# Load and input projection in one program, from unnormalised x, in split fp32r products

## The chip, the cores and the metric

One core of a Trainium2 chip runs the whole kernel in one launch. The metric is the device time of that launch in microseconds, lower is better. TensorE (PE) multiplies; DVE, ACT and POOL are the vector, scalar and GpSimd engines; SP issues transfers.

## The reference, cut to what matters

The kernel computes one decoder layer (attention with three branches beside a state space model, then a gated convolution FFN) for 1024 prompt tokens and 8 sample tokens, all in fp32. The change touches what stands first, the norm and the one input projection of all 1032 tokens:

```python
def rmsnorm(x, g):
    xf = x.astype(jnp.float32)
    y = xf * lax.rsqrt(jnp.mean(xf * xf, axis=-1, keepdims=True) + EPS)
    return (y * g.astype(jnp.float32)).astype(x.dtype)

def project_in(h, w_in):
    z = h @ w_in          # 1024 rows; columns: q 512, kv_c 256, kv_s 256, kv_w 256, gates 24, u 512
...
h = rmsnorm(x, p['norm_mix'])
q, kvc_rows, kvs_rows, kvw_rows, gl, u = project_in(h, p['w_in'])
```

The key/value rows are also results (p_kv_cmp, p_kv_sel, p_kv_win and the same of the samples). Everything after the projection (compression of keys and values, attention, state space scan, output projection, FFN, final norm) is computed by later stages, which the change leaves alone but for the places that they read from.

## The kernel before

The kernel is a row of programs (`nc.Block`), each ending with all engines before the next begins: stage_load, stage_project, stage_compress, stage_attend, stage_turn_attention, stage_ssm, stage_ffn, stage_results (build, at the end). Engines wait on counting semaphores. Each engine's instructions, and each transfer queue's, run in the order in which they are written; nothing is planned by a program.

stage_load: SP loads x in two transfers of 4 token tiles. PE turns each tile of 128 tokens in eight transposes (L184) into PSUM; ACT (L161) and DVE (L204) copy the halves to xT, which holds x with features on the partitions. ACT sums the squares of each token (Square with accumulator, L163), DVE adds and inverts, ACT takes one root for all tiles (Mean.root, L253). Vectors (norms, convolution weights) are turned in L193 and L195.

stage_project: PE spreads the factor of each token over all partitions (Scaling.multiply, L316), ACT keeps it (L322), and DVE makes mixT = xT * gain * factor in eight instructions (Scaling.scale, L328). The jobs then run in the order of JOBS: four query blocks (`q`, weights stationary, three chunks of 344 tokens moving, L473), nine jobs of keys, values and gates (`kv`, tokens stationary, 2 x 396 columns moving, L478), nine of u (`u`, every eighth token stationary, 2 x 256 columns moving, L484). All products are plain fp32. PSUM banks alternate between two groups of four, and ACT and DVE evict half of each job (L588, L531 to L544), so PE waits for the job before the last. Between the jobs the parameters of the state space model are made: small fp32 work on DVE after each eviction (factors, chunk_powers, phases, inputs, weigh_inputs, turns, outputs), the turns of Cin (L495) and Bw (L505) and the kernels K (L519) on PE. SP loads the weights of q and of kv in one transfer each, writes xT to DRAM (x_kept, which the output projection adds later), loads u's weights into the place of q's when the queries are done, and stores the key/value rows tile by tile. E_early, Bw, CW_early and K are spilled to DRAM.

stage_compress: PE turns u (L904), ACT and DVE move it, SP spills it. PE turns rows of the cache (L887) and multiplies them by w_cmp (L896), ACT and DVE move each fill between the two. The rows of a sample come by an indirect transfer from POOL (L877) into one of two tile buffers; the second fetch waits for the spill of u.

The FFN already works with split fp32r products: ACT rounds an operand to fp32r ("upper"), DVE or POOL subtract it from the full value ("rest"), and three products high*high, high*low and low*high stand for one fp32 product (L2455, and L2074 in the state space stage).

## Time and profile before

| | us |
|---|---|
| median of 3 runs (1859.19 to 1865.96) | 1862.39 |
| span of the profiled execution | 1862.2 |
| PE busy | 1730.0 (93%) |
| DVE busy | 942.1 (51%) |
| ACT busy | 564.6 (30%) |
| POOL busy | 351.0 (19%) |
| x turned, PE's first transpose | 9.16 |
| first projection matmul | 36.64 |
| first instruction of PE in stage_compress | 275.03 |

The profile is of one execution. Busy time is the union of an engine's instructions; PEld is the loading of stationary operands, which runs beside the matmuls. A matmul's own duration contains its way through the array, so a stream is read by the distance from start to start, not by the duration of one. An fp32 matmul is recorded as two matmuls.

### The profile page before, as it was taken

Reading aid. Unit: us, or ns where it says so; the run is one execution under the profiler, and the core shown is the slowest. Engines: PE = TensorE matmul, PEld = TensorE weight load, DVE = VectorE, ACT = ScalarE, POOL = GpSimd, SP = SyncE. Lnnn points to the kernel's source line nnn. Section 1 sums busy time; section 2 is a strip of 40 time slices with the busy share of each in tenths; the row PEclk is TensorE's granted clock in tenths of the full one; section 3 lists DMA queues with packets and bytes.
Section 4 is the critical chain, followed back from the end, with each engine's and each line's share of the span. In section 5 each row is a group of like instructions: output and inputs, shape, how many; then the busy total and the mean of one; then the engine's idle time right before and its main releaser. Section 6 shows DMA issues by size and latency. Waiting matters only on the chain. (4 is left out here: it accounts for less than half of the span.)

```text
span 1862.2 us, 27167 instructions
## 1 busy us (share of the span) xinstructions
PE 1730.0 (93%) x10863; PEld 1490.2 (80%) x10864; DVE 942.1 (51%) x1593; ACT 564.6 (30%) x876; POOL 351.0 (19%) x288
## 2 busy tenths in 40 slices
PE   5999999969989998878979899999999999999988
PEld 4655788956555554547979899999999999999978
DVE  3356216776553444119231455655565566556544
ACT  4001115645443444211132332222232222222232
POOL 0000100042213121212125022222222222222210
PEclk8999999979999999797989899999999999999988
DMA  6312516412326134354040111211112112111102
GB/s 241 70 63 77 222 32 227 176 57 62 102 64 214 57 93 179 119 168 148 4 128 1 42 34 40 62 34 59 42 34 68 34 34 68 34 46 55 34 12 97
DMA packets 90684, 155.15 MB, mean 83 GB/s; under 512 B 15302, under 2 KB 68078, under 8 KB 88254
## 3 DMA queue, kind: packets, MB, share of 16 engines
q1 hardware_dynamic: 76736, 93.13, 15.6%
q0 software_dynamic: 13056, 59.77, 9.8%
q10 hardware_dynamic: 816, 1.18, 0.2%
q8 instruction: 54, 0.88, 0.2%
q14 instruction: 22, 0.18, 0.0%
HBM read 133.61 MB, written 24.83 MB: 85 GB/s over the span
## 5 line engine op out<-in xcount | busy, mean ns | idle before, releaser
L2455 PE MATMUL ps<-h_up,w_split 128*128 128x344 f32 x2112 | 399.5, 321 | 7.1 <-DVE h_rest L2617 5.2
L2627 DVE TENSOR_TENSOR xT<-ps,xT 128x688 f32<-128x688 f32 x352 | 228.2, 690 | 283.3 <-PE ps L2455 268.3
L2455 PEld LDWEIGHTS ps<-h_up,w_split 128*128 128x128 f32 x2112 | 345.0, 189 | 8.9 <-DVE h_rest L2617 4.2
L2455 PE MATMUL ps<-gated,wd_split 128*128 128x344 f32 x1584 | 258.3, 321 | 0.9 <-ACT last_row L2569 0.9
L2455 PEld LDWEIGHTS ps<-gated,wd_split 128*128 128x128 f32 x1584 | 251.0, 188 | 1.6 <-issue 1.1
L2455 PE MATMUL ps<-h_rest,w_split 128*128 128x344 f32 x1056 | 224.8, 321 | 0.4 <-ACT wd_split L2565 0.4
L2455 PEld LDWEIGHTS ps<-h_rest,w_split 128*128 128x128 f32 x1056 | 179.1, 189 | 0.7 <-ACT wd_split L2565 0.7
L2581 POOL TENSOR_TENSOR w_split<-w_raw,w_split 128x1024 fp32r<-128x1024 f32 x44 | 114.3, 2598 | 152.4 <-ACT w_split L2527 152.4
L2541 ACT ACTIVATE hu<-ps 128x1032 f32<-128x1032 f32 x44 | 45.4, 1033 | 314.5 <-PE ps L2455 314.5
L2635 DVE SCALAR_TENSOR_TENSOR cv<-hu,ccol,cv 128x1024 f32<-128x1024 f32 x88 | 129.5, 1472 | 16.4 <-ACT cv L2543 10.7
L1719 DVE TENSOR_REDUCE top<-ps 128x1 f32<-128x384 f32 (+4 forms) x124 | 71.1, 585 | 108.1 <-PE ps L1302 63.2
L478 PE MATMUL ps<-w_kvg,mixT 128*128 128x396 f32 (+1 forms) x288 | 96.8, 497 | 0.0
L1623 POOL DMA_INDIRECT unit<-in_cache_kv_sel,rows x64 | 61.1, 955 | 188.1 <-PE ps L1404 97.6
L2602 POOL TENSOR_TENSOR wd_split<-wd_raw,wd_split 128x1024 fp32r<-128x1024 f32 x22 | 54.9, 2496 | 165.5 <-ACT wd_split L2565 165.5
L478 PEld LDWEIGHTS ps<-w_kvg,mixT 128*128 128x128 f32 (+1 forms) x288 | 51.2, 179 | 42.8 <-issue 7.8
L1302 PEld LDWEIGHTS ps<-kT,q_up 128*128 128x128 f32 x336 | 61.5, 201 | 22.6 <-DVE top L1719 6.7
L1302 PE MATMUL ps<-kT,q_up 128*128 128x128 f32 (+3 forms) x336 | 72.7, 306 | 7.1 <-DVE top L1719 2.9
L896 PE MATMUL ps<-rowsT,w_c 128*128 128x128 f32 (+1 forms) x576 | 76.3, 276 | 1.6 <-ACT rowsT L965 1.3
L1335 PE MATMUL ps<-q_up,kT 128*128 128x512 f32 x132 | 69.9, 529 | 3.3 <-ACT prob_win L1543 2.3
L896 PEld LDWEIGHTS ps<-rowsT,w_c 128*128 128x128 f32 x576 | 69.8, 192 | 3.4 <-issue 3.4
L945 DVE COPY rowsT<-ps 64x256 f32<-64x256 f32 (+1 forms) x144 | 59.4, 413 | 22.2 <-PE ps L887 20.1
L484 PE MATMUL ps<-w_qu,mixT 128*128 128x256 f32 (+1 forms) x288 | 70.1, 404 | 0.0
(459 smaller groups left out, 2576.4 us busy)
## 6 DMA issues: line engine op xcount, KB each, us to landing
w_raw<-in_w_up SPq DMA_DIRECT2D x44, 512.0 KB, 6.2
wd_raw<-in_w_down SPq DMA_DIRECT2D x22, 512.0 KB, 3.6
unit<-in_cache_kv_win POOLq DMA_DIRECT2D x16, 512.0 KB, 4.5
x_kept<-xT SPq DMA_DIRECT2D x1, 4128.0 KB, 25.2
xT<-x_kept SPq DMA_DIRECT2D x1, 4128.0 KB
xtok<-in_x_prompt SPq DMA_DIRECT2D x2, 2048.0 KB, 8.2
w_qu<-in_w_in SPq DMA_DIRECT2D x2, 2048.0 KB, 8.7
w_out_sb<-in_w_out SPq DMA_DIRECT2D x4, 1024.0 KB, 11.1
```

What stands on the lines that cost most here:

```text
L478: mm = pe.matmul(k.ps[0:n, bank + c, 0:KVH], hT[:, a, t * P:t * P + n], k.w_kvg[:, a, c * KVH:(c + 1) * KVH], **on)
L484: mm = pe.matmul(k.ps[0:n, bank + c, 0:256], tokens, k.w_qu[:, a, c * 256:c * 256 + 256], **on)
L896: mm = pe.matmul(k.ps[:, 4 + 2 * (j % 2) + h, x * P:x * P + n], k.w_c[:, x, 2 * quad + a].rearrange("p r e -> p (r e)"), k.rowsT[:, f % 4, ...
L945: ins = copy(k.rowsT[HD * s2:HD * s2 + HD, f % 4, h, :, 0:n], rows[:, s2, :, 0:n])
L1302: mm = pe.matmul(out, k.q_up[:, g % 2, h0 + h, :], k.kT[:, br, kvh, b0 * P:(b0 + nb) * P], start=True, stop=b0 not in masks)
L1335: pe.matmul(out, first, k.q_up[:, g % 2].rearrange("p h q -> p (h q)"), start=True, stop=False)
L1623: pool.indirect_dma_start(unit, None, pages, bass.IndirectOffsetOnAxis(ap=k.rows4[:, f, NH2 * n + bb:NH2 * n + bb + 1], axis=0)).then_inc( ...
L1719: dve.tensor_reduce(to, s, AX.X, ALU.max).then_inc(reduced, 1)
L2455: mm = pe.matmul(k.ps[:, bank + c, 0:TG], w(wn), x(xn)[:, c * TG:c * TG + TG], start=start and m == 0, stop=stop and m == 2)
L2581: pool.tensor_tensor(k.w_split[:, z, 1], k.w_raw[:, z], k.w_split[:, z, 0].bitcast(F32), ALU.subtract).then_inc(w_rest, 1)
L2627: dve.tensor_tensor(x[:, part], k.ps[:, bank + part.start:bank + part.stop, 0:TG], x[:, part], ALU.add).then_inc(added, 1)
L2635: dve.scalar_tensor_tensor(k.cv[:, z, 0:SEQ], k.hu[:, z, 1 - n:SEQ + 1 - n], w, k.cv[:, z, 0:SEQ], ALU.mult, ALU.add)
```

## The change

stage_load and stage_project become one program, stage_front. x is loaded tile by tile. When a tile is turned, ACT rounds it from PSUM to fp32r (xh) and DVE subtracts that from PSUM (xl); no xT and no mixT are made. The norm is split: its gain (vcol) goes into the weights, which ACT scales and rounds ("upper") and DVE or POOL complete ("lower"); the factor of each token goes into the evictions, as a scale by partition for kv and u and as a product with the spread factor for the queries. Each tile has its own Square, Sqrt (now with EPS as bias) and reciprocal. Each projection is three fp32r products. Keys and values are cut into three branches of 256, 256 and 280 columns, each over all tiles; the first begins after two tiles are turned, and the turns of the others stand between its jobs. u follows, in one bank of 512 columns a job, with four jobs begun on the first half of the weights; the queries are last. Weight slices share four places, so each is loaded when the branch before that used the place is done. ACT evicts kv and u alone, DVE the queries alone. POOL sums xh and xl and writes the sum to x_kept, eight times, and makes some of the lower parts. DVE makes the state space parameters in one run after the first branch. kv rows are stored four tiles at a time, the window copy of the cache follows the kernels K. stage_compress gets three tile buffers, and its fetches no longer wait for the spill of u. Offsets change, and later stages read kv without the first branch, which has a place of its own (kvc).

```diff
+    R = [k.off_tmp + 8960 * n for n in range(4)]
+
+    def pair(name, parts, width, high, low):
+        hi, _ = at(f"{name}_hi", [P, parts, width], F32R, high)
+        lo, _ = at(f"{name}_lo", [P, parts, width], F32R, low)
+        raw, _ = at(f"{name}_raw", [P, parts, width], F32, low)
+        return hi, lo, raw
+    k.w_kv = [pair(f"w_kv{c}", KD, WIDE[c], R[2 * (c % 2)], R[2 * (c % 2) + 1]) for c in range(3)]
+    k.w_u = [pair(f"w_u{n}", KD // 2, SSMW, R[(2, 0)[n]], R[(3, 1)[n]]) for n in range(2)]
+    q_at = (k.off_kv, R[0], R[1], R[0])
+    k.w_q = [pair(f"w_q{m}", KD, P, q_at[m], q_at[m] + 4096) for m in range(NSAW // P)]
+    k.x_sum, o = at("x_sum", [P, TOK], F32, R[3] + 8960)
+    assert o <= k.off_tail, o
...
+    KV_JOBS = [(c, t) for c in range(3) for t in range(NT + 1)]
+    FIRST_U = len(KV_JOBS)
+    FIRST_Q = len(KV_JOBS) + CH + 1
+    U_BANKS = (0, 1, 2, 4, 5, 6, 0, 1, 2)
+    AHEAD = 4
+    SHORT_AT, C_AT = (0, 5), (1, 0)
+    BT_AT = {(2, x): (2 * x, 2 * x + 1) for x in range(BT_FILLS // 2)}
+    KK_AT = {4 + x: x for x in range(KK_FILLS)}
...
+            xv = k.dram["x_prompt"][0].rearrange("(t p) d -> p t d", p=P)
+
+            def x_tile(t):
+                sp.dma_start(k.xtok[:, t], xv[:, t]).then_inc(x_loaded[t], 16)
+            x_tile(0)
+            for n in range(2):
+                sp.dma_start(k.w_kv[0][2][:, 4 * n:4 * n + 4], wv[:, 4 * n:4 * n + 4, CUT_KV:CUT_KV + KVW]).then_inc(w_in["kv", 0, n], 16)
+            for t in range(1, NT):
+                x_tile(t)
+            sp.dma_start(k.xs[:], k.dram["x_sample"].rearrange("b s d -> (b s) d")).then_inc(x_loaded[NT], 16)
+            sp.dma_start(k.w_kv[1][2][:], wv[:, :, CUT_KV + KVW:CUT_KV + 2 * KVW]).then_inc(w_in["kv", 1, 0], 16)
...
+            sp.wait_ge(left, 4)
+            rows(0, 0, cmp_out)
+            sp.wait_ge(left, 8)
+            rows(0, 4, cmp_out)
+            sp.wait_ge(projected, 9)
+            sp.dma_start(k.w_kv[2][2][:], wv[:, :, CUT_KV + 2 * KVW:CUT_U]).then_inc(w_in["kv", 2, 0], 16)
+            sp.wait_ge(left, 9)
+            sample_rows(0, first_rows)
+            sp.wait_ge(scaling.kept, 1)
+            sp.dma_start(rs_kept, scaling.factor[0:1, 0:SEQ]).then_inc(rs_out, 16)
+            sp.wait_ge(rs_out, 16)
+            sp.dma_start(k.rstd_u[:], rs_kept.rearrange("o (n t) -> (o n) t", t=CH)).then_inc(rs_back, 16)
...
+            sp.wait_ge(projected, 18)
+            sp.dma_start(k.w_u[0][2][:], wv[:, 0:4, CUT_U:CUT_U + SSMW]).then_inc(w_in["u", 0, 0], 16)
...
+            sp.wait_ge(projected, 27)
+            sp.dma_start(k.w_u[1][2][:], wv[:, 4:8, CUT_U:CUT_U + SSMW]).then_inc(w_in["u", 1, 0], 16)
             sp.wait_ge(e_made, 1)
             sp.dma_start(k.e_kept, k.E_early[:].rearrange("p n j c -> p (n j c)")).then_inc(k.e_out, 16)
+            sp.wait_ge(*k.cmp_rows_stored)
+            sp.wait_ge(first_rows, 16)
+            sp.dma_start(k.w_q[0][2][:], wv[:, :, 0:P]).then_inc(w_in["q", 0, 0], 16)
...
+            pe.wait_ge(const_made, 2)
+            turn_x(0)
...
+            turn_x(1)
+            for j, (c, t) in enumerate(Front.KV_JOBS):
+                if c == 0 and t + 2 <= NT:
+                    turn_x(t + 2)
+                if j >= 3:
+                    pe.wait_ge(left, j - 2)
+                if c == 0:
+                    pe.wait_ge(xh_made, min(2 * t + 2, 2 * NT + 1))
+                    pe.wait_ge(xl_made, min(2 * t + 2, 2 * NT + 1))
+                elif t == 0:
+                    pe.wait_ge(w_high, Front.highs("kv", c))
+                    pe.wait_ge(w_low_dve if c == 1 else w_low_pool, Front.lows("kv", c))
...
+                        pe.wait_ge(w_high, a + 1)
+                    tokens, rest = k.xh[:, a, t * P:t * P + n], k.xl[:, a, t * P:t * P + n]
+                    out = k.ps[0:n, j % 3, 0:WIDE[c]]
+                    pe.matmul(out, tokens, high[:, a], start=(a == 0), stop=False)
+                    pe.matmul(out, rest, high[:, a], start=False, stop=False)
+                    if j == 0:
+                        pe.wait_ge(w_low_dve, a + 1)
+                    mm = pe.matmul(out, tokens, low[:, a], start=False, stop=(a == KD - 1))
                 mm.then_inc(projected, 1)
...
+                if (c, t) == (0, NT):
+                    pe.wait_ge(inverted, NT + 1)
+                    scaling.multiply(pe)
...
+            def project_u(t, n):
...
+                    d = 4 * n + a
+                    if t == 0 and n == 1:
+                        pe.wait_ge(w_high, Front.highs("u", 0) + a + 1)
+                        pe.wait_ge(w_low_pool, Front.lows("u", 0) + a + 1)
+                    tokens, rest = [x[:, d, t:SEQ:CH] if t < CH else x[:, d, SEQ:TOK] for x in (k.xh, k.xl)]
+                    pe.matmul(out, tokens, high[:, a], start=(d == 0), stop=False)
+                    pe.matmul(out, tokens, low[:, a], start=False, stop=False)
+                    mm = pe.matmul(out, rest, high[:, a], start=False, stop=(d == KD - 1))
...
+            pe.wait_ge(w_high, Front.highs("u", 0))
+            pe.wait_ge(w_low_pool, Front.lows("u", 0))
+            for t in range(Front.AHEAD):
+                pe.wait_ge(left, Front.FIRST_U - 2 + t if t < 3 else Front.FIRST_U)
+                if t == 3:
+                    pe.wait_ge(scaling.kept, 1)
+                project_u(t, 0)
+            for t in range(CH + 1):
+                if t >= Front.AHEAD:
+                    if t >= 6:
+                        pe.wait_ge(left, Front.FIRST_U + t - 5)
+                    project_u(t, 0)
+                project_u(t, 1).then_inc(projected, 1)
...
+            for m in range(Front.NQ):
+                bank = 4 * (1 - m % 2)
+                high, low, _ = k.w_q[m]
+                pe.wait_ge(w_high, Front.highs("q", m))
+                pe.wait_ge(w_low_dve, Front.lows("q", m))
+                if m < 2:
+                    pe.wait_ge(left, Front.FIRST_U + (6 if m == 0 else CH + 1))
+                else:
+                    pe.wait_ge(q_left, m - 1)
+                for a in range(KD):
+                    for n, (w, x) in enumerate(((high, k.xh), (high, k.xl), (low, k.xh))):
+                        for c in range(3):
+                            mm = pe.matmul(k.ps[:, bank + c, 0:TG], w[:, a], x[:, a, c * TG:c * TG + TG],
+                                           start=(a == 0 and n == 0), stop=(a == KD - 1 and n == 2))
+                mm.then_inc(projected, 1)
...
+            act.wait_ge(ldt_in, 48)
+            act.activation(k.ldt[:], k.ldt[:], ACT.Exp).then_inc(sined, 1)
+            act.wait_ge(to_sine, 1)
+            act.activation(k.PA[:, MAG], k.PA[:, X], ACT.Exp).then_inc(sined, 1)
+            act.wait_ge(to_sine, 2)
+            act.activation(k.PA[:, SIN], k.PA[:, T2], ACT.Sin)
+            act.activation(k.PA[:, T1], k.PA[:, T2], ACT.Sin, scale=0.5).then_inc(sined, 1)
...
+            def root(t):
+                n, x = (P, k.xtok[:, t]) if t < NT else (NB, k.xs[:])
+                act.wait_ge(x_loaded[t], 16)
+                act.activation(k.square[0:n], x, ACT.Square, scale=D_MODEL ** -0.5, accum_out=k.stat[0:n, 0, t:t + 1]).then_inc(summed, 1)
+                act.wait_ge(summed, t + 1)
+                act.activation(k.stat[0:n, 1, t:t + 1], k.stat[0:n, 0, t:t + 1], ACT.Sqrt, bias=k.eps[0:n]).then_inc(rooted, 1)
+
+            def upper(kind, n):
+                high, _, raw = {"kv": k.w_kv, "u": k.w_u, "q": k.w_q}[kind][n]
+                first = KD // 2 * n if kind == "u" else 0
+                for a in range(KD // 2 if kind == "u" else KD):
+                    if a == 0:
+                        act.wait_ge(w_in[kind, n, 0], 16)
+                    if (kind, n) == ("kv", 0) and a == KD // 2:
+                        act.wait_ge(w_in["kv", 0, 1], 16)
+                    act.activation(high[:, a], raw[:, a], ACT.Copy, scale=k.vcol[:, first + a:first + a + 1]).then_inc(w_high, 1)
+                    if kind == "u":
+                        act.activation(raw[:, a], raw[:, a], ACT.Copy, scale=k.vcol[:, first + a:first + a + 1]).then_inc(w_scaled, 1)
+
+            def leave(j, out, src, factor):
+                act.wait_ge(projected, j + 1)
+                act.activation(out, src, ACT.Copy, scale=factor).then_inc(left, 1)
...
+            upper("kv", 0)
+            take_x(1)
+            root(0)
+            act.activation(k.ccol[:], k.ps[:, 7, 32:32 + 8 * NF].rearrange("p (a b) -> p a b", a=4), ACT.Copy).then_inc(vt_kept, 1)
+            for j, (c, t) in enumerate(Front.KV_JOBS):
+                if c == 0:
+                    if t + 2 <= NT:
+                        take_x(t + 2)
+                    if t + 1 <= NT:
+                        root(t + 1)
+                    act.wait_ge(inverted, t + 1)
+                n = P if t < NT else NB
+                to = k.kvc[0:n, t] if c == 0 else k.kv[0:n, t, (c - 1) * KVW:(c - 1) * KVW + WIDE[c]]
+                leave(j, to, k.ps[0:n, j % 3, 0:WIDE[c]], k.stat[0:n, 3, t:t + 1])
+                if (c, t) == (0, 6):
+                    upper("kv", 1)
+                if (c, t) == (0, NT):
+                    scaling.keep(act)
+                if (c, t) == (1, 3):
+                    act.wait_ge(projected, 9)
+                    upper("kv", 2)
...
+                if (c, t) == (2, 4):
+                    upper("u", 0)
+            upper("u", 1)
+            for t in range(CH + 1):
+                j, src = Front.FIRST_U + t, k.ps[0:(P if t < CH else NB), Front.U_BANKS[t], :]
+                if t == 0:
+                    act.wait_ge(k.e_out, 16)
+                    act.wait_ge(rs_back, 16)
+                if t < CH:
+                    leave(j, k.U[:, :, CH - 1 - t, :], src.rearrange("p (g c) -> p g c", c=GC), k.rstd_u[:, t:t + 1])
+                else:
...
+                if t == 3:
+                    upper("q", 0)
...
+            for m in range(1, Front.NQ):
+                if m == 3:
+                    act.wait_ge(projected, Front.FIRST_Q + 2)
+                act.dma_start(k.w_q[m][2][:], wv[:, :, m * P:m * P + P]).then_inc(w_in["q", m, 0], 16)
+                if m == 2:
+                    for n in (1, 2):
+                        upper("q", n)
+            upper("q", 3)
...
+            def lower_kv():
+                high, low, raw = k.w_kv[2]
+                pool.wait_ge(w_high, Front.highs("kv", 2))
+                for a in range(KD):
+                    pool.tensor_scalar(raw[:, a], raw[:, a], k.vcol[:, a:a + 1], None, ALU.mult).then_inc(lane_made, 1)
+                for a in range(KD):
+                    pool.wait_ge(lane_made, a + 2)
+                    pool.tensor_tensor(low[:, a], raw[:, a], high[:, a].bitcast(F32), ALU.subtract).then_inc(w_low_pool, 1)
+
+            def lower_u(n):
+                high, low, raw = k.w_u[n]
+                for a in range(KD // 2):
+                    pool.wait_ge(w_scaled, 4 * n + a + 1)
+                    pool.tensor_tensor(low[:, a], raw[:, a], high[:, a].bitcast(F32), ALU.subtract).then_inc(w_low_pool, 1)
+
+            def keep_x(a):
+                pool.wait_ge(xl_made, 2 * NT + 1)
+                if a:
+                    pool.wait_ge(x_spilled, 16 * a)
+                pool.tensor_tensor(k.x_sum[:], k.xh[:, a].bitcast(F32), k.xl[:, a].bitcast(F32), ALU.add).then_inc(x_summed, 1)
+                pool.wait_ge(x_summed, a + 1)
+                pool.dma_start(k.x_kept[:, a * TOK:a * TOK + TOK], k.x_sum[:]).then_inc(x_spilled, 16)
+            for a in range(3):
+                keep_x(a)
+            lower_kv()
+            for a in range(3, 6):
+                keep_x(a)
+            lower_u(0)
+            for a in range(6, KD):
+                keep_x(a)
+            lower_u(1)
             pool.wait_ge(cw_made, 1)
...
-                                      ).then_inc(kk_added, 1)
-            for a in range(KD):
...
+            def lower(kind, n):
+                high, low, raw = (k.w_kv if kind == "kv" else k.w_q)[n]
+                for a in range(KD):
+                    dve.wait_ge(w_high, Front.highs(kind, n) - KD + a + 1)
+                    dve.scalar_tensor_tensor(low[:, a], raw[:, a], k.vcol[:, a:a + 1], high[:, a].bitcast(F32),
+                                             ALU.mult, ALU.subtract).then_inc(w_low_dve, 1)
...
             angles()
-            leave(dve, dve.tensor_copy, 1, left_dve, after)
-    k.rows_stored = (rows_out, n_rows_out[0])
-    k.stores.append(k.rows_stored)
+            take_x_rest(0)
+            lower("kv", 0)
+            take_x_rest(1)
+            invert(0)
+            for n in range(NT + 1):
+                if n + 2 <= NT:
+                    take_x_rest(n + 2)
+                if n + 1 <= NT:
+                    invert(n + 1)
+                if n in (1, 2, 3):
+                    factors(n - 1)
+            lower("kv", 1)
+            chunk_powers()
+            phases()
+            inputs()
+            weigh_inputs(0)
+            weigh_inputs(1)
+            for first, last in ((0, 3), (3, 5), (5, 6), (6, 7)):
+                turns(first, last)
+            outputs(0)
+            outputs(1)
...
+            dve.wait_ge(scaling.kept, 1)
+            lower("q", 1)
+            lower("q", 2)
...
+    k.tile = [at(f"tile{n + 1}", [P, SUB, 2 * NKV, HD], F32, (k.off_mix, k.off_mix + 16384, 9216 + 16384)[n])[0] for n in range(3)]
...
+                if j >= 4:
+
+                    pool.wait_ge(transposed, FILLS * (j - 2))
+                pool.indirect_dma_start(k.tile[b % 3][:].rearrange("n s c d -> n (s c d)"), None, rows,
```

## Rows read from the trace of the kernel before

**Rows 1.** By stretch: length, busy PE, PEld, DVE, ACT, POOL; clock, transfer share, GB/s.

```profile
20.00:36.60 16.60, 3.74 (x19) 3.50 (x18) 4.00 (x5) 10.10 (x17) 0.12 (x1) 0.63 0.46 159
36.60:97.40 60.80, 60.76 (x231) 40.20 (x231) 25.83 (x79) 6.39 (x9) 0.00 (x0) 0.96 0.44 126
97.40:197.00 99.60, 99.60 (x322) 54.81 (x321) 63.02 (x116) 8.57 (x16) 0.93 (x2) 1.00 0.24 90
197.00:275.00 78.00, 77.25 (x417) 70.49 (x417) 6.37 (x18) 8.18 (x18) 4.75 (x7) 1.00 0.33 116
```

**Rows 2.** Timeline of TensorE before 50 us: start, length, what, count.

```profile
9.16 9.51 PE L184 MATMUL ps<-ident,xtok 128*128 128x128 f32 x64 [9.16 <-DMA xtok<-in_x_prompt]
...
36.64 2.09 PE L473 MATMUL ps<-mixT,w_qu 128*128 128x344 f32 x3 [4.76 <-DMA w_qu<-in_w_in]
```

**Rows 3.** Timeline of TensorE, the projections, to the start of stage_compress.

```profile
67.40 28.03 PE L473 MATMUL ps<-mixT,w_qu 128*128 128x344 f32 x96
95.36 2.16 PE L495 MATMUL ps<-ident,Cin 16*128 16x16 f32 x32
...
129.47 1.04 PE L505 MATMUL ps<-ident,Bw 128*128 128x128 f32 x8
130.34 10.81 PE L478 MATMUL ps<-w_kvg,mixT 128*128 128x396 f32 x32
...
206.81 8.02 PE L484 MATMUL ps<-w_qu,mixT 128*128 128x256 f32 x32
...
216.62 8.02 PE L484 MATMUL ps<-w_qu,mixT 128*128 128x256 f32 x32
...
236.23 38.02 PE L484 MATMUL ps<-w_qu,mixT 128*128 128x256 f32 x160
275.03 3.68 PE L904 MATMUL ps<-ident,U 128*128 128x128 f32 x32 [0.78 <-PEq L393]
```

**Rows 4.** Timeline of TensorE, fp32r products in attention and in the gated unit.

```profile
459.94 0.39 PE L1339 MATMUL ps<-q,k 128*128 128x512 f32 x1
460.17 0.34 PE L1302 MATMUL ps<-kT,q_up 128*128 128x256 f32 x2
...
901.11 0.63 PE L2074 MATMUL ps<-g_rest,w_glu_up 128*128 128x344 f32 x3
901.58 0.62 PE L2074 MATMUL ps<-g_up,w_glu_rest 128*128 128x344 f32 x3
```

**Rows 5.** Timeline of TensorE in stage_compress: turns and products of one fill.

```profile
296.06 1.06 PE L896 MATMUL ps<-rowsT,w_c 128*128 128x128 f32 x8
296.95 0.60 PE L887 MATMUL ps<-ident,tile 128*128 128x128 f32 x4
297.39 1.06 PE L896 MATMUL ps<-rowsT,w_c 128*128 128x128 f32 x8
```

**Rows 6.** Weight loads of u by shape: count, busy us, mean ns, idle before.

```profile
L484 PEld LDWEIGHTS ps<-w_qu,mixT 128*128 128x128 f32 x256 | 61.6, 337 | 1.5 <-issue 1.5
```

**Rows 7.** Groups of ACT by shape: count, busy us, mean ns, idle before.

```profile
L163 ACT ACTIVATE square<-xtok 128x1024 f32<-128x1024 f32 x8 | 8.4, 1049 | 0.0
...
L161 ACT ACTIVATE xT<-ps 128x512 f32<-128x512 f32 x8 | 4.8, 598 | 0.2
...
L253 ACT ACT_TABLE_LOAD x3 | 3.8, 1283 | 0.1
```

**Rows 8.** Groups of DVE by shape: the eviction of the queries.

```profile
L531 DVE COPY qT<-ps 64x1032 f32<-64x1032 f32 x4 | 4.9, 1234 | 32.1 <-PE ps L473 32.1
```

**Rows 9.** Groups of POOL by shape: a subtraction of 512 columns.

```profile
L1578 POOL TENSOR_TENSOR q<-qT,q_up 64x512 fp32r<-64x512 f32 x16 | 20.2, 1262 | 83.3 <-ACT q_up L1471 83.1
```

**Rows 10.** Page, transfers: count, KB each, median us to landing.

```profile
unit<-in_cache_kv_win POOLq DMA_DIRECT2D x16, 512.0 KB, 4.5
...
w_qu<-in_w_in SPq DMA_DIRECT2D x2, 2048.0 KB, 8.7
```

**Rows 11.** Waits, 275 to 382 us: us in total, times, longest.

```profile
PE ps L887 <- DMA tile<-in_cache_kv_cmp,rows_of: 3.0, 2, 1.9
```

669 lines of the change are left out of this document (301 added, 368 removed).

## The prediction

> **What bounds the kernel now.** I read the busy time by stretch first [rows 1]. Only the time before 275 us is touched in earnest. There TensorE is the bound: from 36.6 to 275 us it is busy for 237.6 of 238.4 us, while DVE, ACT and POOL are mostly idle. Before that it mostly waits: from 20 to 36.6 us it is busy for 3.7 us, and its clock is there partly at the lower of its two levels (1.2 of 2.4 GHz), for the mean granted clock is 0.63. Second, the timeline of TensorE [rows 2] names what those 36.6 us are: x turned from 9.16 us on, then the norm's factor, the scaled copy mixT, and a wait for w_qu. The first projection matmul is at 36.64. Third, the timeline of the projections [rows 3] gives pitches. The evictions lie beside them: jobs follow each other without a gap. The attention, the output projection and the FFN keep their instructions, so I leave their time alone.
>
> So the front costs 275.0 us, from the start to TensorE's first instruction of stage_compress [rows 3], and I build the same interval for the changed kernel. The profiled span, 1862.2 us, is 0.2 us below the median of the runs, 1862.4, so one sum serves for both.
>
> **Prices.** A plain fp32 product is recorded as two matmuls, each with two passes. The 344 wide one takes 28.03/96 = 0.292 us a record, the 396 wide one 10.81/32, some 0.335, and the 256 wide one of the u part 38.8/160, some 0.24 us (236.23 to 275.03) [rows 3]. Split fp32r products replace each of them with three matmuls of one pass. Three fp32r matmuls of 344 columns start 0.47 us apart, 0.157 each, and one of 512 columns is followed by the next after 0.23 us [rows 4]. Both are 0.45 to 0.46 ns a column, so I take 0.12 us for 256 columns and 0.131 for 280. The lower bound is 0.111, the pitch of matmuls with as much streaming (128 columns in two passes) and a weight load each [rows 5]: 8 of them in 0.89 us. The upper bound is 0.13.
>
> The u part has a stride of 8 tokens in its stationary operand. Its weight load is 337 ns long [rows 6], and by the 396 wide records its 256 wide ones should take 0.335 x 256/396 = 0.217 us, but they take 0.24. I read the strided load as the bound there, and I keep 0.24 us for the 512 wide fp32r matmul, which alone would need 0.23. Its bounds are 0.23 and 0.28.
>
> The Trainium skill puts a weight load at the number of columns over 1.2 GHz, some 107 ns, whatever the stride (TensorE: Matmul & The Clock Gate, section LDWEIGHTS). By that page the u part would be bound by its columns and cost 2 us less. This trace speaks against it, with 337 ns against 107, so the sum doesn't use it.
>
> **The change part by part.**
> First job ready. x tile 0 is now a transfer of 0.5 MB, not 2, so its turns begin near 5 us instead of 9.16. But the small vectors and the ssm parameters come over ACT's queue (11 issues, the last near 5.5 us), and ACT does Exp, Exp, Sin, Sin before it takes tile 0. I put the first scaled weight slice at 12.5 us (bounds 10 and 16); ACT and DVE then deliver a slice each 0.45 us, so job 0 ends near 16.5. The 28 us of norm, mixT and weight wait ahead of the first product are gone: the norm's factor is only needed at the evictions.
>
> First branch (kvc). Job 1 starts near 17.5, when ACT has taken tile 1. A job has 24 matmuls of 0.12, 2.9 us, and the turns of a later tile, 8 x 0.11 = 0.9 us [rows 5]: 3.8 us. ACT has per tile two takes, a Square with its accumulator, a Sqrt and an eviction: 2 x 0.6 + 1.05 + 0.19 + 0.3 + 0.45, some 3.2 us [rows 7]. So TensorE is just the bound. Jobs 1 to 5 take 19, job 6 3.5, job 7 2.9, the job of 8 samples 2.7, and the parameter turns 0.5: the branch ends at 46.
>
> Spreading the factor, 18 records at the upper clock: 2. Second branch: 8 x 2.88 + 2.7 = 25.7, and the 32 turns of Cin 2.1 [rows 3]. Third branch, 280 wide: 8 x 3.14 + 3.1 = 28.2. The turns of Bw cost 0.87 a pair of fills (129.47 to 130.34), 3.5 in all; they are moved, not new. The u part: 192 x 0.24 + 24 x 0.23 = 51.6, and four kernel fills of 2.15 (a u job with its fill starts 9.81 after the one before, from 206.81 to 216.62, and 32 records of 0.24 are 7.66), 8.6 [rows 3]. The queries: 4 x 72 x 0.158 = 45.5; these were 56 and cost four fifths now. At the end DVE alone evicts the last queries, two instructions of 1.23 [rows 8], and the program's end adds 0.4: 3.0, where before it was 0.8.
>
> Sum: 46 + 2 + 25.7 + 2.1 + 28.2 + 3.5 + 51.6 + 8.6 + 45.5 + 3.0 = 216.2.
>
> Seams. Each weight slice is loaded, scaled and split before its branch, and I follow each. For the third branch ACT has the upper part at 66 us. POOL then scales and subtracts 8 slices; at 1262 ns for 512 columns [rows 9] that is 0.7 each for the subtraction, and 0.3 to 0.7 for the scaling: it ends at 74 to 78, needed at 76. For the second half of u the load starts only when job 27 ends. 2 MB took 8.7 us and 0.5 MB 4.5 [rows 10], so it lands after 5 to 8; its four slices need 2.5 more for the first and 1.3 for each that follows. The four u jobs run ahead on the first half cover 11.5: nothing, or up to 3. For query block 1 the load goes out on ACT's queue with the 4 MB copy of the window cache in flight; block 0 covers it for 11.4 us: 0 to 5. POOL's new work (eight sums of x of 2.5 us, each with a transfer waited for, 7 us a piece) lies ahead of its splits on its queue. It begins near 38 us and is clear of them by 56, so it costs nothing while that cover holds; if each took 12 us the last split would be 4 us late. DVE's parameter work (63 us busy of 99.6 from 97.4 on, evictions included [rows 1], and some 10 before) loses its evictions and runs unbroken from 45 us: Bw by 73 us (needed at 79), CW by 118 (needed at 145). SP's waits in order (for jobs 9, 18, 27) hold nothing that is needed sooner. I add 1.5 us for the seams, bounds 0 and 12.
>
> stage_compress. With three tile buffers the fetches no longer wait for the spill of u; TensorE's waits for tiles are 3.0 us [rows 11]. I take 2 of them back (bounds 3 and -1).
>
> Result: 275.0 - 216.2 - 1.5 + 2 = 59.3 us less, **1803 us**.
>
> **Rivals.**
> Table loads. Sqrt now stands between Squares, tile by tile. The trace shows a load of 1283 ns before each Sqrt [rows 7]; it shows Square and Copy under three different tables without a load, and Copy under Sqrt's, but never Square under Sqrt's. If Square isn't there, ACT has two loads per tile, 5.8 us against TensorE's 3.8: 2 us for each of 7 or 8 tiles, 15 us, **1818 us**. Square's use under each other table speaks against it: 12%.
> The Trainium skill says to finish all calls of one table set before the next, and counts cheap functions as members of every set without naming Square (ScalarE: Activation LUTs, section Table sets: the hidden batching unit). Its rule, applied to the letter, is this rival.
>
> Late splits. POOL's sums of x, POOL's slower scaling, and the loads that start only at a branch's end are each at the bad bound: 4 + 3 + 5 us and less cover from one to the next. TensorE then stands at the starts of the third branch, the second half of u and query block 1. That is 10 us over the forecast, **1813 us**: 13%.
>
> Clock. TensorE is now fed by ACT and DVE tile by tile, and in this trace a stretch with such gaps ran at a mean of 0.63 [rows 1]. At the lower level all pitches double. The gain is gone when 59 us of matmul time run there, that is all of the first branch (27 us) and the second and a part of the third. Fully kept up to the end of the third branch, 27 + 26 + 28 us are added to the forecast: **1884 us**, slower than before. Against it: branches two and three wait for no tile, and the timeline shows the upper level soon after the products start (0.96 from 36.6 on): 3%.
>
> The change doesn't do what it says: three matmuls of one pass cost no less than two records of two passes if the pitch were bound by the load. For 256 columns this is already nearly so (24 x 0.12 for 256 columns against 32 x 0.335 for 792); with 0.14 instead of 0.12 the kv part would cost 8 us more, 1811 us, inside the range.
>
> **How the numbers follow.** The forecast, 1795 to 1813 on its own, has 69%, table loads 12%, late splits 13%, the clock 3%, and 3% is for what I don't see. The range takes in the first three with their bounds: **1795 to 1824**. A measurement of this kernel can tell 0.3%, 5.6 us, from no change. Faster by more than that: 0.95; within it: 0.02; slower: 0.03.
>
> **What would show it.** TensorE's first instruction of the compression stage at 216 to 220 us, not 275. Pitches of 0.12 (256 columns), 0.24 (u) and 0.158 (queries). ACT's table loads before 60 us: three, or some twenty. TensorE's idle time before the first matmul of the third branch, of u's second half and of query block 1: near nothing. If the stages behind 275 us change by more than 3 us in all, something that I left alone has moved. I am wrong if the first job ends after 22 us, if the u part costs more than 65 us with its fills, or if the granted clock is below 0.9 between 20 and 100 us.

## The result, and the profile after

The changed kernel takes 1857.45 us (median of 14 runs, 1850.79 to 1864.63), the kernel before 1864.16 us in the same sessions (14 runs). The ratio is 0.9963, with a 95% interval of 0.9953 to 0.9974: some 7 us less, where 59 us less were forecast. The forecast of 1803 us and its range of 1795 to 1824 us are both wrong. The profiled execution has a span of 1853.9 us, against 1862.2 us before.

TensorE's first instruction of stage_compress is at 268.44 us (before: 275.03, rows 3; forecast: 217.7, that is 216.2 and 1.5 for the seams). What lies behind it is 1585.5 us long, against 1587.2. So the missing gain is all in the front, and most of it lies in three waits and in the lower clock behind them. The waits of TensorE ahead of 275 us, in the changed kernel (us in total, times, longest):

```profile
PE ps L548 <- ACT w_q_hi L596: 19.3, 1, 19.3
PE ps L477 <- POOL w_kv_lo L703: 11.1, 1, 11.1
PE ps L514 <- POOL w_u_lo L709: 6.9, 4, 5.2
PE ps L453 <- DMA crow<-in_conv_b: 5.7, 1, 5.7
PE ps L425 <- DMA xtok<-in_x_prompt: 4.8, 1, 4.8
PE ps L1095 <- PEq L323: 2.8, 1, 2.8
PE ps L477 <- DVE w_kv_lo L894: 1.4, 1, 1.4
```

L477 is the first product of a kv job, L514 that of a u job, L548 the queries, L1095 the first turn of stage_compress. The same stretch by windows (length, busy TensorE, granted clock, transfer share, GB/s), which answers to rows 1:

```profile
80.00:100.00 20.00, 8.91 (x51) 0.66 0.31 106
100.00:140.00 40.00, 37.26 (x249) 1.00 0.52 191
140.00:160.00 20.00, 15.84 (x44) 0.66 0.54 169
...
200.00:220.00 20.00, 10.31 (x66) 0.82 0.67 216
220.00:240.00 20.00, 10.44 (x55) 0.67 0.26 49
```

A stretch of 20 us mixes the wait with what follows it. In stretches of 5 us (length, busy TensorE, granted clock, transfer share, GB/s) the work behind the waits is seen by itself:

```profile
90.00:95.00 5.00, 3.69 (x16) 0.50 0.02 6
...
150.00:155.00 5.00, 5.00 (x13) 0.52 0.88 324
155.00:160.00 5.00, 5.00 (x22) 1.00 0.98 242
```

From 230 to 235 us, behind the third wait, the granted clock is 0.67, and from 235 us on 1.00. So each of the three waits is followed by a stretch at the lower clock. How it looks in the timeline of TensorE (start, length, what, count, idle time before and its releaser), at the edges of the stretches:

```profile
48.49 2.33 PE L211 MATMUL ps<-ident,stat 128*128 128x128 f32 x18
52.25 0.36 PE L477 MATMUL ps<-w_kv_hi,xh 128*128 128x256 f32 x1 [1.43 <-DVE w_kv_lo L894]
...
91.31 0.57 PE L477 MATMUL ps<-w_kv_hi,xh 128*128 128x280 f32 x1 [11.09 <-POOL w_kv_lo L703]
...
125.23 0.51 PE L514 MATMUL ps<-w_u_hi,xh 128*128 128x512 f32 x1
...
198.79 0.63 PE L548 MATMUL ps<-xh,w_q_hi 128*128 128x344 f32 x3
...
229.56 1.20 PE L548 MATMUL ps<-xh,w_q_hi 128*128 128x344 f32 x3 [19.25 <-ACT w_q_hi L596]
...
234.66 0.64 PE L548 MATMUL ps<-xl,w_q_hi 128*128 128x344 f32 x3
```

From these edges the forecast's sum can be settled term by term:

| stretch | forecast | measured | over |
|---|---|---|---|
| start to the end of the first branch | 46 | 48.49 | 2.5 |
| factor spread, to branch 2 | 2 | 3.76 | 1.8 |
| branch 2 with Cin (to 80.22) | 27.8 | 27.97 | 0.2 |
| wait before branch 3 | in the seams | 11.09 | 11.1 |
| branch 3 with Bw | 31.7 | 33.92 | 2.2 |
| u with the kernel fills | 60.2 | 73.56 | 13.4 (6.9 idle) |
| queries and end | 48.5 | 69.65 | 21.1 (19.3 idle) |

The excess is 52.2 us, less the 1.5 us that the forecast had for seams: 50.7. Waits in the seams are 37.3 of it. What is left in the last three rows beside their waits is 2.2 + 6.5 + 1.8 = 10.5 us. Of it 1.4 are u's own price (in e10_kk_later, below, where the clock stays up, u takes 62.7 us with 1.1 of wait, 1.4 over the forecast); 9.1 lie at the lower clock behind the waits. 4.4 us are ahead of all that; 1.4 of them are TensorE's wait for DVE's lower part of the second branch, for which the forecast had no term.

### The profile page after: what moved, and what is told of

Read it like the earlier page. It is cut to its first block and busy times, and to the rows that moved or that the text cites. A ratio compares the mean times of both kernels' runs of the same rounds, so it can differ in the third digit from the quotient of the medians.

```text
span 1853.9 us, 28106 instructions
## 1 busy us (share of the span) xinstructions
PE 1692.8 (91%) x11248; PEld 1513.0 (82%) x11248; DVE 976.0 (53%) x1635; ACT 604.5 (33%) x978; POOL 412.8 (22%) x328
## 3 DMA queue, kind: packets, MB, share of 16 engines
q1 hardware_dynamic: 78610, 87.32, 15.3%
q0 software_dynamic: 14208, 64.00, 10.3%
## 5 line engine op out<-in xcount | busy, mean ns | idle before, releaser
L1493 PEld LDWEIGHTS ps<-kT,q_up 128*128 128x128 f32 x336 | 62.0, 202 | 23.4 <-DVE top L1910 6.4
L477 PE MATMUL ps<-w_kv_hi,xh 128*128 128x256 f32 (+3 forms) x216 | 64.2, 297 | 12.5 <-POOL w_kv_lo L703 11.1
L2776 POOL COPY last<-hu 128x10 f32 (+1 forms) x44 | 8.5, 192 | 292.1 <-ACT hu L2732 292.1
L1526 PE MATMUL ps<-q_up,kT 128*128 128x512 f32 x132 | 70.1, 531 | 3.1 <-ACT prob_win L1734 2.3
L2752 ACT ACTIVATE gated<-cv 128x1032 fp32r<-128x1032 f32 x22 | 23.5, 1070 | 148.4 <-DVE cv L2844 148.4
L1136 DVE COPY rowsT<-ps 64x256 f32<-64x256 f32 (+1 forms) x144 | 59.4, 413 | 20.3 <-PE ps L1078 18.3
## 6 DMA issues: line engine op xcount, KB each, us to landing
w_out_sb<-in_w_out SPq DMA_DIRECT2D x4, 1024.0 KB, 11.1
```

Of the source, the lines that this page charges most:

```text
L477: pe.matmul(out, tokens, high[:, a], start=(a == 0), stop=False)
L1136: ins = copy(k.rowsT[HD * s2:HD * s2 + HD, f % 4, h, :, 0:n], rows[:, s2, :, 0:n])
L1493: mm = pe.matmul(out, k.q_up[:, g % 2, h0 + h, :], k.kT[:, br, kvh, b0 * P:(b0 + nb) * P], start=True, stop=b0 not in masks)
L1526: pe.matmul(out, first, k.q_up[:, g % 2].rearrange("p h q -> p (h q)"), start=True, stop=False)
```

## The experiments

All edits are made to the changed kernel; times are compared with the kernel before, run on the same chip. The clearest measure is where stage_compress starts in the profile, since what lies behind it differs little (1582.5 to 1592.8 us in all but e12_warm_all, where it is 1603.8). Where a kernel has one run, its time alone settles little: the changed kernel's 14 runs lie up to 7 us from their median. The starts are of one profile each, and the wait in u differs between kernels whose edit doesn't touch it (6.9, 7.0 and 8.2 us, but 3.4 in e9_late_crow and 4.1 in e1_copy_early). So a start is put down to an edit only as far as the wait that the edit aims at has changed.

| kernel | start | wait, branch 3 | wait, u | wait, queries | new waits | median (ratio, interval) |
|---|---|---|---|---|---|---|
| changed | 268.4 | 11.1 | 6.9 | 19.3 | | 1857.5 (0.9963, 0.9953 to 0.9974) |
| e1_copy_early | 247.6 | 10.4 | 4.1 | 0 | bt_stage 5.1 | 1838.8 (0.9865, 0.9833 to 0.9897) |
| e2_tile0_late | 260.3 | 10.4 | 6.9 | 12.1 | | 1847.2, one run |
| e11_copy_behind | 251.7 | 10.2 | 8.2 | 2.6 (block 3) | | 1840.7, one run |
| e3_split_dve | 249.1 | 0 | 0.2 | 19.0 | Bw 4.3, CW 0.5 | 1838.4 (0.9875, 0.9837 to 0.9914) |
| e4_act_scales | 250.0 | 5.1 | 0.7 | 18.3 | | 1840.4, one run |
| e5_dve_quiet | 265.3 | 3.7 | 0 | 19.1 | Bw 15.3 | 1859.8, one run |
| e6_pool_order | 259.7 | 10.2 | 2.2 | 19.5 | | 1846.5 (0.9905, 0.9873 to 0.9937) |
| e9_late_crow | 261.8 | 10.9 | 3.4 | 19.5 | | 1846.4, one run |
| e7_warm | 267.7 | 2.1 | 7.0 | 19.4 | | 1857.1 (0.9949, 0.9932 to 0.9966) |
| e12_warm_all | 259.4 | 0.4 | 0 | 1.3 | | 1856.8 (0.9955, 0.9935 to 0.9975) |
| e8_three | 230.4 | 0 | 0.9 | 0 | CW 6.2 | 1817.8 (0.9750, 0.9722 to 0.9777) |
| e10_kk_later | 223.2 | 0 | 1.1 | 0 | | 1811.1 (0.9739, 0.9716 to 0.9763) |

### The wait before query block 1

SP issues the 4 MB copy just before the loads of w_q1 and w_q2. SP's and ACT's timelines in the changed kernel:

```profile
195.10 0.82 SPq L399 DMA_DIRECT2D out_s_kv_win<-in_cache_kv_win  x1
...
201.74 13.15 SPq L407 DMA_DIRECT2D tile<-out_p_kv_cmp  x1
```

```profile
199.00 1.05 ACTq L664 DMA_DIRECT2D w_q_raw<-in_w_in  x2
226.63 2.45 ACT L596 ACTIVATE w_q_hi<-w_q_raw,vcol 128x128 fp32r<-128x128 f32 x8 [26.96 <-DMA w_q_raw<-in_w_in]
```

The 512 KB of w_q1 need 27.6 us, where 512 KB took 4.5 us in rows 10. SP's own instruction for the tile's fetch takes 13.15 us here, and 0.54 in e1_copy_early, where the copy isn't just ahead of it. Three orders of the same transfers were tried.

e1_copy_early:

```
             sample_rows(1, rows_out)
+            sp.dma_start(k.dram["s_kv_win"][0, :, 0:WIN - 1].rearrange("b t a h d -> b t (a h d)"),
+                         k.dram["cache_kv_win"][0, :, 1:WIN].rearrange("b t a h d -> b t (a h d)")).then_inc(cache_out, 16)
...
-            sp.dma_start(k.dram["s_kv_win"][0, :, 0:WIN - 1].rearrange("b t a h d -> b t (a h d)"),
-                         k.dram["cache_kv_win"][0, :, 1:WIN].rearrange("b t a h d -> b t (a h d)")).then_inc(cache_out, 16)
             sp.wait_ge(projected, Front.FIRST_Q)
```

> Edit to the changed kernel: SP issues the 4 MB copy of the window cache behind the store of the samples' second rows (near 81 us) and not behind the last kernel store (195 us). Theory 'copy': in the changed kernel the load of w_q1, issued at 199.0 us, lands at 226.6 us because the copy, issued at 195.1, is ahead of it on the same 16 DMA engines. Then w_q1 now lands 4 to 8 us after its issue, TensorE's idle time of 19.3 us before query block 1 falls to 0 to 3, and the block runs at the full clock from its start (1.5 to 2 us more). Together 18 to 22 us less than the changed kernel: 1836 to 1840 us, a ratio of 0.985 to 0.987 to the kernel before. Rival 'tile': the 1 MB fetch of the first tile of stage_compress (issued at 201.7) and its small pe_cmp rows are what w_q1 shares the engines with; then it still lands after 15 us or more, the idle time stays above 10, and the gain is under 10 us. Second rival 'moved': the copy, now beside the load of w_u0, the x sums' spills and bt's stores, costs as much there, in the third branch or the first half of u; then the query seam is gone and the time is not less.

e2_tile0_late:

```
-            sp.wait_ge(projected, Front.FIRST_Q)
+            sp.wait_ge(projected, Front.FIRST_Q + 3)
```

> Edit to the changed kernel: SP waits for three query blocks, not for the last u job, before it fetches the first tile of stage_compress (four pe_cmp loads and 1 MB of rows). The copy of the window cache stays where it is. Theory 'copy': w_q1 still lands 12 us or more after its issue and TensorE still waits 5 us or more before query block 1. Rival 'tile': w_q1 lands 4 to 8 us after its issue, the idle time is 0 to 3, and the time falls by 18 to 22 us. In between, if both loads share the engines evenly with w_q1: landing after 14 to 18 us, idle 6 to 10, which would say that the 27 us were the sum of both. The tile itself is needed near 250 to 268 us and comes in time if it lands within 10 us.

e11_copy_behind:

```
-            sp.dma_start(k.dram["s_kv_win"][0, :, 0:WIN - 1].rearrange("b t a h d -> b t (a h d)"),
-                         k.dram["cache_kv_win"][0, :, 1:WIN].rearrange("b t a h d -> b t (a h d)")).then_inc(cache_out, 16)
             sp.wait_ge(projected, Front.FIRST_Q)
...
                          k.dram["p_kv_cmp"][0, 0].rearrange("(n s) x h d -> n (s x h d)", s=SUB)).then_inc(k.prompt_in, 16)
+            sp.dma_start(k.dram["s_kv_win"][0, :, 0:WIN - 1].rearrange("b t a h d -> b t (a h d)"),
+                         k.dram["cache_kv_win"][0, :, 1:WIN].rearrange("b t a h d -> b t (a h d)")).then_inc(cache_out, 16)
```

> Edit to the changed kernel: the copy of the window cache is issued behind the fetch of the first tile, near 202 us, so that the loads of w_q1 and w_q2 (issued at 199.0) are in the queues ahead of it. Theory 'ahead': a load waits for what was given to the same 16 DMA engines before it, not for what comes after. Then w_q1 lands 4 to 8 us after its issue though the copy runs at the same time, the 19.3 us of wait before query block 1 are gone, and the time falls by 15 to 22 us. Rival 'beside': the engines divide themselves between all queues, so that w_q1 again lands 12 us or more after its issue whenever the copy is in flight. w_q3, issued near 222, may land late by the copy's rest in both cases (up to 5 us before block 3).

ACT's first split of w_q1 in e1_copy_early, in e2_tile0_late and in e11_copy_behind, with its wait for the load, and in the first and the last of them also that of w_q2, whose load was issued 0.45 us behind w_q1's:

```profile
203.47 2.46 ACT L596 ACTIVATE w_q_hi<-w_q_raw,vcol 128x128 fp32r<-128x128 f32 x8 [3.40 <-DMA w_q_raw<-in_w_in]
207.60 2.46 ACT L596 ACTIVATE w_q_hi<-w_q_raw,vcol 128x128 fp32r<-128x128 f32 x8 [1.68 <-DMA w_q_raw<-in_w_in]
```

```profile
218.54 3.61 ACT L596 ACTIVATE w_q_hi<-w_q_raw,vcol 128x128 fp32r<-128x128 f32 x12 [19.81 <-DMA w_q_raw<-in_w_in]
```

```profile
203.34 2.45 ACT L596 ACTIVATE w_q_hi<-w_q_raw,vcol 128x128 fp32r<-128x128 f32 x8 [3.57 <-DMA w_q_raw<-in_w_in]
207.65 2.45 ACT L596 ACTIVATE w_q_hi<-w_q_raw,vcol 128x128 fp32r<-128x128 f32 x8 [1.86 <-DMA w_q_raw<-in_w_in]
```

With the copy issued at 82 us, w_q1 lands 4.1 us after its issue, in the company of the tile's fetch. With the copy ahead and the tile's fetch out of the way it takes 20.5 us; the fetch adds 7. With the copy issued 3.4 us behind it, it takes 4.2 us; but then it had only 0.8 us to go, so this says little against 'beside'. The load of w_q2 says more: it had 5.2 us to go when the copy was issued, and landed after 8.1 us, against 7.7 in e1_copy_early. So for these loads 'ahead' holds and 'beside' falls: what counts is what was issued before. The third load, w_q3, shows the same from the other side: in e11_copy_behind it is issued 19.3 us behind the copy and takes 11.0 us, against 3.7 to 3.8 in the others. Whether a load behind the copy moves nothing until the copy is through, or only a small share, these runs do not tell. 'moved' came true in part: in e1_copy_early bt's stores stand behind the copy, and TensorE waits 5.1 us for bt_stage. The query part alone (from its first matmul to stage_compress) shrank from 69.65 to 48.4 us, the 48.5 of the forecast.

Order of issue is not the whole account of a landing. The spill of the seventh sum of x (516 KB, issued by POOL) landed after 10.3 us in the changed kernel, though the 2 MB store of E was issued 0.9 us behind it, with the 1 MB load of w_u1 1.1 us ahead. In e12_warm_all, where that store came 9.7 us behind the spill, it landed within 3.

### The wait before the third branch

POOL's timeline in the changed kernel, and DVE's in the same time:

```profile
70.11 15.19 POOL L700 TENSOR_SCALAR w_kv_raw<-w_kv_raw,vcol 128x280 f32<-128x280 f32 x8 [7.97 <-ACT w_kv_hi L596]
85.27 5.89 POOL L703 TENSOR_TENSOR w_kv_lo<-w_kv_raw,w_kv_hi 128x280 fp32r<-128x280 f32 x8
```

```profile
69.24 2.29 DVE L837 TENSOR_TENSOR early_tmp<-pw,Bb 128x2048 f32<-128x2048 f32 x1
71.57 2.47 DVE L838 TENSOR_TENSOR Bw<-early_tmp 128x2048 f32<-128x2048 f32 x1
...
85.10 0.19 DVE L2053 TENSOR_TENSOR early_tmp<-E_early,ph 128x32 f32<-128x32 f32 x1
85.33 0.76 DVE L2054 TENSOR_TENSOR E_early<-early_tmp 128x32 f32<-128x32 f32 x1
...
88.33 0.68 DVE L2052 TENSOR_TENSOR pt<-ph 128x16 f32<-128x16 f32 x1
```

POOL's first scalings are as long as DVE's products, and DVE's tiny instructions (0.17 to 0.19 us alone) become nearly as long as POOL's subtractions (5.89/8 = 0.74) as soon as these begin. e3_split_dve takes POOL out, e4_act_scales takes its scaling out, and e5_dve_quiet takes DVE away from it.

e3_split_dve:

```
-    BT_AT = {(2, x): (2 * x, 2 * x + 1) for x in range(BT_FILLS // 2)}
+    BT_AT = {(2, x + 1): (2 * x, 2 * x + 1) for x in range(BT_FILLS // 2)}
...
-                if (c, t) == (1, 3):
+                if (c, t) == (1, 1):
                     act.wait_ge(projected, 9)
                     upper("kv", 2)
...
-            lower_kv()
...
             inputs()
+            lower("kv", 2)
             weigh_inputs(0)
```

> Edit to the changed kernel: the third branch's upper part is made by ACT behind job (1, 1), not (1, 3), and its lower part by DVE in one instruction a slice ahead of the first weigh_inputs, not by POOL in two; the turns of Bw go out a job later. Theory 'POOL split': TensorE's 11.1 us before the third branch are POOL's 21 us for the lower part alone. DVE needs 8 x 0.5 = 4 us (66.9 to 71), so the third branch starts at 80 us at the full clock: 11.1 + 2.1 us less, 1843 to 1846 us, ratio 0.988 to 0.991. Bw is ready 4 us later (86 us) and needed only after job (2, 1), at 86.5: 0 to 1 us of wait. Rival 'DVE is late instead': DVE's chain of Bw, E and CW is pushed back, and TensorE waits as long for Bw (before the turns) or CW (before the first kernel fill): the time changes by under 4 us and the idle time is put down to DVE's Bw or CW.

e4_act_scales:

```
-                    if kind == "u":
+                    if kind == "u" or (kind, n) == ("kv", 2):
                         act.activation(raw[:, a], raw[:, a], ACT.Copy, scale=k.vcol[:, first + a:first + a + 1]).then_inc(w_scaled, 1)
...
                 for a in range(KD):
-                    pool.tensor_scalar(raw[:, a], raw[:, a], k.vcol[:, a:a + 1], None, ALU.mult).then_inc(lane_made, 1)
-                for a in range(KD):
-                    pool.wait_ge(lane_made, a + 2)
+                    pool.wait_ge(w_scaled, a + 1)
                     pool.tensor_tensor(low[:, a], raw[:, a], high[:, a].bitcast(F32), ALU.subtract).then_inc(w_low_pool, 1)
```

> Edit to the changed kernel: for the third branch ACT also writes the scaled slices, as it does for u, so that POOL only subtracts. Theory 'price': the third branch starts late because POOL's scaling costs 1.35 us a slice where the forecast had 0.3 to 0.7. Then POOL's eight subtractions of 0.74 end near 75 us and TensorE has no wait at 80. Theory 'turns with DVE': where both engines work, each POOL instruction waits until DVE's is done and the other way round; in the changed kernel POOL's first four scalings took 2.3 to 2.5 us each, just as long as DVE's 2048 element products (2.29 alone, 2.47 beside POOL), and only the last four, beside short ones, 1.35. Then the subtractions take 2.3 to 3.1 us each while DVE makes Bw (67 to 84 us), the last ends at 82 to 87, TensorE waits 2 to 7 us, and DVE's six products of Bw take 2.8 to 3.1 us each, not 2.3 to 2.5.

e5_dve_quiet:

```
             inputs()
+            dve.wait_ge(w_low_pool, KD)
             weigh_inputs(0)
```

> Edit to the changed kernel: DVE waits for POOL's lower part of the third branch before it begins Bw, so that POOL works alone. Theory 'turns with DVE': POOL's scalings take 1.35 us each from the first on, 8 x 1.35 + 8 x 0.74 = 16.7 us from 70.1, and the third branch starts at 86 to 87 us, not 91.3. Theory 'price': the first four scalings take 2.3 to 2.5 us as before and the branch starts at 91. With both at work the 21 us of the changed kernel divide into 16.7 of POOL's own price (forecast 8.0 to 11.2) and 4.4 of turns with DVE. Bw is then 15 us later and TensorE waits for it at the first turns of Bw, some 10 us, so the time as a whole is longer; that is the cost of the experiment and not part of its question.

POOL in e5_dve_quiet, alone:

```profile
70.27 7.72 POOL L700 TENSOR_SCALAR w_kv_raw<-w_kv_raw,vcol 128x280 f32<-128x280 f32 x8 [9.36 <-ACT w_kv_hi L596]
77.97 5.93 POOL L703 TENSOR_TENSOR w_kv_lo<-w_kv_raw,w_kv_hi 128x280 fp32r<-128x280 f32 x8
```

POOL and DVE in e4_act_scales, both at work:

```profile
67.14 17.59 POOL L700 TENSOR_TENSOR w_kv_lo<-w_kv_raw,w_kv_hi 128x280 fp32r<-128x280 f32 x8 [5.32 <-ACT w_kv_raw L598]
```

```profile
66.37 2.29 DVE L833 TENSOR_TENSOR early_tmp<-pw,Bb 128x2048 f32<-128x2048 f32 x1
68.70 2.76 DVE L834 TENSOR_TENSOR early_tmp<-pw,Bb 128x2048 f32<-128x2048 f32 x1
71.50 2.77 DVE L835 TENSOR_TENSOR Bw<-early_tmp 128x2048 f32<-128x2048 f32 x1
```

Alone, POOL needs 0.97 us a scaling and 0.74 a subtraction, 13.7 us in all; beside DVE it needed 21.1. My expectation had taken 1.35 us for the scaling alone; even those four had shared. With the scaling gone but DVE at work, the eight subtractions still take 17.6 us. They are not alike: the first takes 2.2 us, the next five 2.82 to 2.84, one for each of DVE's products, and the last two, beside DVE's tiny instructions, 0.77. DVE's products take 2.76 and not 2.29. So both parts are shown: 'price' is worth 2.5 to 5.7 us over the forecast's 8.0 to 11.2, 'turns with DVE' 7.4 us. Either alone left TensorE waiting: 3.7 us in e5_dve_quiet, 5.1 in e4_act_scales. The times by which I had measured this had both moved by 4 us: POOL began at 70.1 us and not at 66, and the branch was needed at 80.2 and not at 76, so these two cancel. e5_dve_quiet pays for its quiet with 15.3 us of wait for Bw, where some 10 were expected.

The Trainium skill has this rule (SBUF — State Buffer, section SBUF: two separate sides): DVE and GpSimd share one pair of ports as an exclusive lock, which a DVE instruction with two inputs in SBUF and a GpSimd instruction that reads SBUF each hold to their end. The trace agrees for the subtractions: DVE's 0.17 us became 0.70 beside a subtraction of 0.74, and in e4_act_scales one subtraction went with each product. For the scalings it agrees only in part: one went with each of DVE's products, but the product took 2.47 us, and not its own 2.29 and the scaling's 0.97 one after the other. The forecast let both engines run beside each other at full speed, and did not weigh this rule.

e3_split_dve gained more than was expected (19.3 us in the front, not 13.2), since POOL, freed of the third branch, was also on time for u. It brought a wait of its own for Bw, 4.3 us where 0 to 1 was expected.

### The waits in u

ACT had the first slice of w_u1 scaled at 132.6 us. POOL's timeline around it, in the changed kernel:

```profile
126.50 0.57 POOL L717 DMA_DIRECT2D x_kept<-x_sum  x1 [0.30 <-POOL x_sum L715]
136.91 3.19 POOL L715 TENSOR_TENSOR x_sum<-xh,xl 128x1032 f32<-128x1032 f32 x1 [9.83 <-DMA x_kept<-x_sum]
...
140.99 7.95 POOL L709 TENSOR_TENSOR w_u_lo<-w_u_raw,w_u_hi 128x512 fp32r<-128x512 f32 x4
```

POOL stands before its eighth sum until the seventh has been spilled, and the split is queued behind. The four subtractions then take 7.95 us beside DVE's products, and not the 5.0 of four times 1.26 (rows 9). e6_pool_order:

```
-            for a in range(6, KD):
-                keep_x(a)
             lower_u(1)
+            for a in range(6, KD):
+                keep_x(a)
```

> Edit to the changed kernel: POOL splits the second half of w_u before the last two sums of x, not behind them. Theory 'queue': the 6.9 us that TensorE waits in u (5.2, then 3 x 0.57) come from POOL's queue, where the spill of the seventh sum takes 9.8 us to land beside the load of w_u1 and the 2 MB store of E; ACT has the first slice of w_u1 scaled at 132.6, and POOL only starts on it at 141.0. Now it starts at 132.6, and with 2.2 us a slice (as these subtractions take while DVE works) it has the four at 133.7, 136, 138 and 140.5; TensorE needs them at 137.1 and then every 0.73: idle time 0 to 2 us, and the 14 us at the lower clock behind it go too (6 us). 10 to 13 us less: 1844 to 1848 us, ratio 0.990 to 0.992. Rival 'load': the load of w_u1 and ACT's scaling end last and TensorE still waits 3 us or more: under 5 us less.

The wait fell from 6.9 to 2.2 us and stage_compress started 8.8 us sooner; the ratio of 0.9905 is inside what was expected. 'queue' holds.

### The start of the front

e9_late_crow:

```
-            pe.wait_ge(vec_loaded, 8 * 16)
-            pe.transpose(k.ps[:, 7, 0:32], k.vrow[:], k.ident[0:32, 0:32])
+            pe.wait_ge(vec_loaded, 4 * 16)
+            pe.transpose(k.ps[:, 7, 0:32], k.vrow[:], k.ident[0:32, 0:32]).then_inc(vt_ready, 1)
+            turn_x(1)
+            pe.wait_ge(crow_in, 4 * 16)
...
-            turn_x(1)
```

> Edit to the changed kernel: the turns of the convolution vectors (crow) get a semaphore of their own and come behind the turn of tile 1, so that TensorE turns the norm vectors as soon as those four small loads have landed. The profile puts TensorE's 5.7 us ahead of them down to the load of conv_b, landed near 12.4 us. Theory 'ACT': that wait hides another one, ACT's Exp, Exp, Sin and Sin with two table loads, which ends at 11.9 us; ACT takes tile 0 until 12.9 and would then only be 0.5 us sooner at the first weight slice: the first product moves from 16.6 to 16.1 us, the time stays (within 1 us). Rival 'crow': the load is what binds, and the first product comes 4 us sooner, near 12.5 us.

The first product moved from 16.62 to 15.65 us: 1.0 us, not 4. The 5.7 us of wait that the profile puts down to crow hid another one, for ACT. All the same stage_compress started 6.7 us sooner, so the expectation that the time stays was missed: the waits in u were 3.4 us and not 6.9. The trace shows where this comes from. The seventh sum's spill, issued at 126.3 us (126.5 in the changed kernel), held POOL for 4.0 us and not 9.8; the load of w_u1 was issued 2.0 us ahead of it and not 1.1, the store of E 0.9 us behind it in both. No run varies that distance alone, so the cause is not shown.

### The clock behind the waits

In e7_warm and e12_warm_all TensorE is given matmuls that nobody reads where it waited; the work is added, and none is left out. The lines of the first, which stand behind job (1, NT); the second has them with 92 there, and in bank 7 with 42 and 3 x 4 in u and 158 before query block 1:

```
+                    for _ in range(72):
+                        pe.matmul(k.ps[:, 5, 0:256], k.xh[:, 0, 0:P], k.xh[:, 1, 0:256], start=True, stop=True)
```

> Edit to the changed kernel: behind the last job of the second branch TensorE does 72 more matmuls of 256 columns into a bank that nobody reads (8.5 us of work that fills its wait for the third branch's lower part). Theory 'clock': the stall costs more than its 11.1 us, for after it TensorE's granted clock is 0.5 for some 5 us and 24 matmuls of 280 columns take 0.233 us each, not 0.130. With the wait filled, the clock stays at the upper level or near it, the third branch still starts at 91 us, and it ends 1.5 to 2.5 us sooner: the time falls by 2 us, a ratio of 0.994 to 0.996 to the kernel before. Rival 'load or turn': the slow pitch after the stall is something else (weights just written, Bw's turns); then the first job keeps 0.233 and the time stays.

> Edit to the changed kernel, after the first try with one wait filled (there 2.1 us of the wait were left, the granted clock still fell to 0.74 from 90 to 95 us, and the third branch's first job took 4.6 us, not 5.5; upper level 3.1): now all three waits are filled with matmuls of 256 columns into a bank that nobody reads, 92 before the third branch (10.8 us), 42 and 3 x 4 before the four slices of u's second half (4.9 and 0.5 us), 158 before query block 1 (18.6 us). The waits themselves stay, for no cause of them is touched. Theory 'clock': by the changed kernel's rows the time lost behind the waits is 2.4 us in the third branch (its first job takes 5.5 us, not 3.1), 6.4 in u (13.3 over the forecast, 6.9 of it idle) and 2.0 in query block 1 (its first 4.15 us do work of 2.1), 10.8 in all. With the clock kept up, 7 to 11 us of that come back: stage_compress starts at 258 to 262 us, not 268.4, and the time is 1847 to 1851, a ratio of 0.990 to 0.993. Rival: the filler only moves the loss (it takes as long as the waits, ends late by 1 to 2 us each, or the throttle takes the clock back elsewhere): start at 265 or later, time within 3 us of the changed kernel.

In e7_warm, with 2.1 us of the wait left, the granted clock was 0.74 in the 5 us behind it and the first job took 4.6 us: 0.8 us of the front came back, where 1.5 to 2.5 were expected. In e12_warm_all the granted clock stayed at 1.00 up to 250 us and stage_compress started at 259.4 us, 9.1 us sooner, as expected for the front. In u the filler covered no wait: the seventh spill landed within 3 us there, POOL had all four slices by 135.8 us, and TensorE went through its filler until 139.6 with the first of them ready. As that filler is about as long as the wait was (54 matmuls at 0.12 us against 6.9 us), the comparison of the two fronts still stands. But the time did not fall to the 1847 to 1851 us that were expected. Windows of e12_warm_all:

```profile
80.00:100.00 20.00, 19.62 (x164) 1.00 0.35 117
140.00:160.00 20.00, 20.00 (x98) 1.00 0.43 135
210.00:240.00 30.00, 28.65 (x207) 1.00 0.35 63
260.00:285.00 25.00, 23.71 (x142) 0.59 0.86 337
```

and the same work in the changed kernel:

```profile
269.00:294.00 25.00, 22.22 (x212) 1.00 0.86 336
```

So in this profile the first 25 us of stage_compress ran at 0.59 though TensorE was busy for 23.7 of them. stage_compress, up to TensorE's first instruction of the next stage, took 113.2 us and not 105.5; another 10.6 us were lost further back, which no run explains. Nor is the filler shown to be what brought the clock down: in e5_dve_quiet, which has none, the granted clock was 0.66 from 265 to 290 us, with TensorE busy for 23.4 us, and stage_compress took 111.5. The profiled execution was also the longest of its kernel (1864.9 us, of 1851.0 to 1864.9). What is shown: with TensorE kept busy in their place the front is 9.1 us shorter, which is what the sum above puts on the lower clock behind the waits. Whether keeping the upper clock there is a gain for the whole program stays open; the two filled kernels show none.

### The mends together

e8_three has e3_split_dve and e6_pool_order, the copy behind the samples' first rows, Bw's turns at (2, x + 2), and ACT's scaling of w_u0 one job later. e10_kk_later adds:

```
-    KK_AT = {4 + x: x for x in range(KK_FILLS)}
+    KK_AT = {5 + x: x for x in range(KK_FILLS)}
```

> The changed kernel with the three seams mended together: the window cache's copy issued at 50 us behind the store of the samples' first rows, the third branch split by ACT behind job (1, 1) and by DVE, with Bw's turns two jobs later, and POOL's split of the second half of w_u ahead of its last two sums of x. If the missing gain lay in the three waits and the clock after them, TensorE's first instruction of stage_compress comes at 222 to 228 us (the changed kernel 268.4, the forecast 217.7), the times add (19.3 + 20.8 us of the single edits measured there, 3 more for Bw): 1809 to 1817 us, a ratio of 0.971 to 0.976 to the kernel before. If a new wait takes the place of an old one (CW before the first kernel fill, bt_stage's stores behind the copy, w_u1's load), the start is above 232 us and the time above 1822.

> The combination of three mends with the kernel fills behind u's jobs 5 to 8, not 4 to 7. In the combination TensorE waited 6.2 us for DVE's CW before the first kernel fill (142.5 to 148.7) and the matmuls behind it ran at the lower clock (32 records of the fill in 3.5 us, where 1.9 is usual). One u job is 5.9 us, so the wait falls to under 1 us and the clock stays up: the compression starts at 221 to 224 us, not 230.4, and the time falls by 7 to 9 us more, to 1808 to 1812 us, ratio 0.970 to 0.972. Rival: the last fill now lies at the end of u and ACT's two copies of it delay the loads of w_q1 and w_q2 by 1 to 3 us; if that shows as a wait before query block 1, the gain is under 5 us.

In e8_three DVE's CW became the new wait (6.2 us); DVE now makes the lower part of the third branch ahead of Bw and CW. The start of 230.4 us lies outside the 222 to 228 that were expected, and short of the rival's 232. One u job more of cover removed it: what is left of waits in the front of e10_kk_later, beside 2.8 us at its end and 1.4 before the second branch, is

```profile
PE ps L453 <- DMA crow<-in_conv_b: 5.5, 1, 5.5
PE ps L425 <- DMA xtok<-in_x_prompt: 4.9, 1, 4.9
...
PE ps L514 <- POOL w_u_lo L709: 1.1, 1, 1.1
```

and stage_compress starts at 223.18 us:

```profile
223.18 1.10 PE L1095 MATMUL ps<-ident,U 128*128 128x128 f32 x6 [2.83 <-PEq L323]
```

That is 45.3 us sooner than in the changed kernel and 5.5 us behind the forecast: 4.4 up to the end of branch 2, 1.4 for u's price and 1.1 for its wait, less the 1.5 us of the seams. The kernel takes 0.9739 of the time before, interval 0.9716 to 0.9763, and beats both: 2.6% less against 0.4%. The place of stage_compress and the median (1811.1 us) are inside what was expected; the ratio is short of its 0.970 to 0.972, though the interval reaches it.

## Why the prediction was wrong

**Prices: right.** 256 columns 0.12 us, 280 columns 0.129 and 344 columns 0.158 are as taken; the second branch took 27.97 us for 27.8. Only u's 512 columns are 0.246, not 0.24, which makes 1.4 us with the fills. Three fp32r matmuls do cost what was taken, so this rival falls. The strided weight load takes 329 to 333 ns, near the 337 of the trace of before (rows 6).

**Table loads: right.** ACT's groups up to 268 us have three loads; the last is the only one for the square root:

```profile
L563 ACT ACT_TABLE_LOAD x1 | 1.3, 1283 | 6.0 <-issue 6.0
L567 ACT ACT_TABLE_LOAD x1 | 1.3, 1283 | 0.0
L586 ACT ACT_TABLE_LOAD x1 | 1.3, 1283 | 0.0
```

Square and Sqrt stand nine times each, and the one load is ahead of the first Sqrt. The Trainium skill has cheap functions in every table set and doesn't name Square among them (ScalarE: Activation LUTs, section Table sets: the hidden batching unit). In this trace Square does not need a set of its own, so the rival falls.

**First branch: 2.5 us off.** It ended at 48.5, not 46; the first product came at 16.6 us where the first slice was put at 12.5. The first job ended at 20.3 us and not near 16.5, and the jobs behind it made up a part.

**Seams: the step that failed.** I took 1.5 us with an upper bound of 12; the waits were 37.3. Three terms were mis-sized.
- Query block 1, 0 to 5 us against 19.3. I priced the load of w_q1 by its own size and named the copy in flight without pricing it. Rows 10 had the number: 2048 KB took 8.7 us, so 4 MB ahead of it are some 17 us, and the tile's 1 MB another 4 to 5. 17.4 + 4.4 + 4.5 of its own, less the copy's lead of 3.9 and the cover of 11.4, is a wait of 11 us: an estimate from these rows, and a term too large to leave at the middle of its bounds. The measured wait adds 5.2 us to the landing and 2.9 us from there until ACT and DVE had split the block, which I had left out.
- Third branch, -2 to 2 us against 11.1. The slice of the scaling is 0.97 us, not 0.3 to 0.7, and I added POOL's and DVE's times as if they could run beside each other. They take turns, 7.4 us more here. No row that I took from the trace of before had both engines long at work on SBUF at once, and I did not ask what that lack meant.
- u's second half, 0 to 3 us against 6.9. I gave a sum of x with its spill 7 us and wrote that the sums would be clear of the splits by 56 us. That can only hold for the three sums ahead of the third branch's split; two others stand right before the split of u's second half, and of these I had only said what 12 us each would cost. The seventh took 14.1 us (122.81 to 136.91): 3.4 for the sum and 10.4 until its spill, issued among the load of w_u1 and the store of E, had landed. In e12_warm_all, with that store 9.7 us later, sum and spill took 5.8 us. The order on POOL's queue was followed to the first split, not to the last.

**Clock: named, priced in the wrong place.** I gave it 3% as a rival over whole branches. It came as 9.1 us behind the three waits. The line "wrong if the granted clock is below 0.9 between 20 and 100 us" did catch it: 0.66 from 80 to 100.

**Late splits** was the rival with the right mechanism, at 13% and 1813 us. It was held to the bad bounds of the three terms, and these were too low by a factor of three.

**stage_compress: right.** 2 us were taken for it; 1.7 us came behind the start of stage_compress, and TensorE's waits for tiles fell by as much, from 3.0 to 1.3 us.

## What to carry to other kernels

Here a load took 4.1 us by itself and 20.5 with 4 MB issued just ahead of it; so before a load is moved behind a compute stage, list what the queues hold at that moment, in bytes. DVE, with two operands in SBUF, and POOL did one subtraction for each product; in stretches where both work their times are to be added, not laid beside each other, which is a little too much for POOL's scalings. Where a change makes one engine's stream denser, each wait that is left costs its idle time and, as the waits of 11.1, 5.2 and 19.3 us did here, a piece at the lower clock; so sum the seams at their bad bounds first: they, not the prices, decide what a well-priced saving is worth.

## What the runs showed of the hardware

- DVE and POOL took turns instruction by instruction: a DVE instruction of 16 columns took 0.70 us beside POOL's subtractions and 0.17 alone.
- A POOL multiplication by a per-partition scalar, 280 columns of fp32 in SBUF, takes 0.97 us alone; a subtraction of two such operands 0.74 alone and 2.82 to 2.84 beside DVE products of 2048 columns.
- 512 KB landed in 4.1 us by themselves, in 20.5 us with 4 MB issued 3.9 us ahead, and in 27.6 us with 1 MB more beside. With the 4 MB issued 3 us behind, the load took 8.1 us and not 7.7.
- TensorE was at its lower clock level after each of its waits of 11.1, 5.2 and 19.3 us. With matmuls in place of the waits it was at 1.00 there, and then at 0.59 in a stretch of 25 us where it was busy for 23.7; without them, in another kernel, at 0.66 in such a stretch.
